# Strassen blocks of a float32 decoder trunk: three of the seven block products go through one PSUM bank, with the tokens' high and low parts in one 512-column matmul

## The chip, the cores and the metric

The kernel runs on one core of a Trainium2 chip. The metric is the device time of one execution in microseconds (us), the median over several runs; what is compared is the kernel before and the kernel with the change.

## What is computed

A causal decoder trunk with 512 tokens of width 1024, in float32. Four SwiGLU feed-forward stages stand around an attention and pooling mixer and an mLSTM mixer. The change touches the feed-forward stages alone, and in them the first two of the three matrix products:

```python
D_MODEL, SEQ = 1024, 512
D_FF = 256 * ((8 * D_MODEL // 3 + 255) // 256)     # 2816

def swiglu(x, w_gate, w_up, w_down):
    return (jax.nn.silu(x @ w_gate) * (x @ w_up)) @ w_down

x = x + FFN_RESIDUAL * swiglu(rms_norm(x, gain), w_gate, w_up, w_down)    # 4 times in the trunk
```

## The kernel before, in words

Features lie on the partitions and tokens along the free dimension. Every float32 operand is split into a high part and the rest (fp32r), and a product is the sum of three: high weight by high token, high weight by low token, low weight by high token. A plain product of a 128x1024 weight tile with 512 tokens is 8 x 3 matmuls of 512 columns.

D_FF is 22 tiles of 128 rows (`FT`). The first `PLAIN` of them in each stage (5, 4, 3, 3 in the four stages) are computed plainly. The other 17 + 18 + 19 + 19 = 73 go through `block(p)`: the pair (up tile p, gate tile p) is a 2 x 2 block matrix (up and gate by left and right half of the input features) and the tokens are cut into two halves of 256. Strassen's scheme in Winograd's form makes the four result quarters from seven products instead of eight, each of 4 feature tiles x 3 matmuls with 256 columns, 84 matmuls in all. The seven are called one, five, six, seven, three, and two plain ones for the right halves of up and gate. Sums of weights (`ASR`, split into `ASH` and `ASL`) are made ahead by an accumulating DMA that GpSimd issues (`add_pair`) and by VectorE (`sums_second`, `sums_third`, `sums_split`). Sums of tokens are in `BF` and `BFL`.

Between the products quarter results have to be added up. Before the change, ScalarE copies product one out of PSUM (`copy_one`), VectorE adds the others to it on the way to the small buffer MID (`mid_two`, `mid_five`, `mid_three`), and adds MID onto the up bank and the gate bank (`whole_up`, `whole_gate`). TensorE has the next product in other banks meanwhile.

Around a block stand these steps. ScalarE copies the high part of the next weights (`split`: HI<-RING, 1024 columns, then 512) and of the next sums (`sums_split`: ASH<-ASR, twice), and of a piece of the down weights (`early_split`: DHI<-DRAW). VectorE makes the low parts behind it (LO, ASL, DLO). When the block is done VectorE multiplies by the norm factor (`gate`), ScalarE applies Silu (`silu`), GpSimd multiplies again, VectorE multiplies by the up bank (`up`), ScalarE copies the high part (`h_high`: HH<-TMP), and GpSimd makes the low part. Behind most blocks TensorE runs `early(p)`: a part of the down product, 24 matmuls of 512 columns, or 18 with the first four pieces of stages two to four. It needs DHI and DLO of that block. The stages have 16 such pieces each. Block 15 of the third and fourth stage (`ALONE`) has none behind it, nor have the blocks 20 and 21 of stages two to four, nor block 21 of the first.

The order on each engine is written out by hand in the program, with semaphores between the engines. An engine carries out its own list in order, so an instruction that waits holds up all behind it.

## Time and profile before

| | |
|---|---|
| median of 3 runs | 1956.07 us (1955.17 to 1956.20) |
| span of the profiled execution | 1954.0 us |
| PE busy | 1948.1 us (100%), 11722 matmuls |
| VectorE (DVE) busy | 1397.9 us (72%) |
| ScalarE (ACT) busy | 851.6 us (44%) |
| GpSimd (POOL) busy | 527.3 us (27%) |
| granted TensorE clock | 1.000 |

The span reaches from the first to the last instruction of one profiled execution. The profile gives no other time for that execution, so the 2.1 us between the span and the median of the runs are what lies around it. A busy share is an average over all stages, and a matmul's recorded duration overlaps the next one's, so TensorE's pace is read from the starts of its matmuls.

### The profile page before, as it was taken

How to read it: one execution, taken by the hardware profiler on the slowest of the kernel's cores; microseconds unless marked ns; L12 is line 12 of the kernel's file. 1: busy time of each engine (PE TensorE's matmuls, PEld its weight loads, DVE VectorE, ACT ScalarE, POOL GpSimd, SP SyncE). 2: the span in 40 equal slices, each digit the busy share in tenths (PEclk: the TensorE clock that was granted, in tenths of full speed). 3: DMA queues.
4: the chain of work that ended last, by engine and by line, in shares of the span. 5: the costliest groups of instructions: out<-in, count | busy, mean ns of one | idle time of the engine just before them, and what ended most of it. 6: DMA issues, size and time to landing. Idle time of an engine off the chain costs nothing.

```text
span 1954.0 us, 28996 instructions
## 1 busy us (share of the span) xinstructions
PE 1948.1 (100%) x11722; PEld 1707.3 (87%) x11722; DVE 1397.9 (72%) x1882; ACT 851.6 (44%) x1230; POOL 527.3 (27%) x394
## 2 busy tenths in 40 slices
PE   9999999999999999999999999999999999999999
PEld 7999998877789999988999998877777888999997
DVE  7877776554588877768877776773458657877773
ACT  6443333535554344345433444442546345333431
POOL 1322222142223322223322322200015413322221
PEclk9999999999999999999999999999999999999999
DMA  6556663351346666545666653232200235666653
GB/s 211 155 164 171 173 168 95 119 181 55 88 126 176 174 172 167 147 129 145 178 166 172 181 151 114 97 96 88 76 1 1 87 116 160 177 173 168 178 141 107
DMA packets 112469, 265.92 MB, mean 136 GB/s; under 512 B 10321, under 2 KB 22865, under 8 KB 112337
## 3 DMA queue, kind: packets, MB, share of 16 engines
q1 hardware_dynamic: 92336, 225.72, 35.3%
q0 software_dynamic: 19856, 38.28, 12.5%
q8 instruction: 93, 1.52, 0.3%
q14 instruction: 40, 0.32, 0.0%
q10 hardware_dynamic: 144, 0.09, 0.0%
HBM read 259.32 MB, written 4.72 MB: 135 GB/s over the span
## 4 chain that ended last, share of the span: by engine, by line
PE 98%; DVE 1%; DMA 0%; issue 0%; ACT 0%; SPq 0%; POOL 0%; DVEq 0%
PE BANKS L656 12%; PE BANKS L658 12%; PE BANKS L657 12%; PE BANKS L579 11%; PE BANKS L580 11%; PE BANKS L581 11%; PE BANKS L709 6%; PE BANKS L710 6%; PE BANKS L711 6%; PE BANKS L1022 2%; PE BANKS L850 1%; PE BANKS L852 1%; PE BANKS L851 1%; PE BANKS L999 1%; PE BANKS L1005 1%; PE BANKS L813 1%
## 5 line engine op out<-in xcount | busy, mean ns | idle before, releaser
L656 PE MATMUL BANKS<-BF,ASH 128*128 128x256 f32 x876 | 248.0, 283 | 0.0
L658 PE MATMUL BANKS<-BF,ASL 128*128 128x256 f32 x876 | 247.9, 283 | 0.0
L657 PE MATMUL BANKS<-BFL,ASH 128*128 128x256 f32 x876 | 247.9, 283 | 0.0
L579 PE MATMUL BANKS<-XH,HI 128*128 128x512 f32 x624 | 245.7, 394 | 0.7 <-DVE XL L1593 0.3
L1657 DVE TENSOR_TENSOR LO<-RING,HI 128x1024 fp32r<-128x1024 f32 (+2 forms) x204 | 216.3, 1060 | 41.2 <-ACT HI L1160 39.9
L580 PE MATMUL BANKS<-XL,HI 128*128 128x512 f32 x624 | 243.2, 390 | 0.0
L581 PE MATMUL BANKS<-XH,LO 128*128 128x512 f32 x624 | 243.0, 389 | 0.0
L1173 ACT ACTIVATE TMP<-TMP 128x512 f32<-128x512 f32 x88 | 55.7, 633 | 406.4 <-DVE TMP L1686 406.4
L2262 POOL TENSOR_TENSOR TMP<-TMP,RSTD 128x512 f32<-128x512 f32 x88 | 132.0, 1499 | 365.3 <-ACT TMP L1173 365.3
L2254 POOL DMA_DIRECT2D ASR<-gu_dram x73 | 88.1, 1219 | 387.5 <-DMA ASR<-gu_dram 381.5
L709 PE MATMUL BANKS<-HH,DHI 128*128 128x512 f32 x488 | 190.7, 391 | 0.0
L710 PE MATMUL BANKS<-HL,DHI 128*128 128x512 f32 x488 | 190.6, 391 | 0.0
L1160 ACT ACTIVATE HI<-RING 128x1024 fp32r<-128x1024 f32 (+2 forms) x204 | 171.4, 876 | 42.3 <-DMA RING<-down_dram 21.4
L711 PE MATMUL BANKS<-HH,DLO 128*128 128x512 f32 x488 | 189.8, 389 | 0.0
L1676 DVE TENSOR_TENSOR ASL<-ASR,ASH 128x1024 fp32r<-128x1024 f32 x146 | 181.6, 1246 | 0.0
L2264 POOL TENSOR_TENSOR HL<-TMP,HH 128x512 fp32r<-128x512 f32 x88 | 139.0, 1580 | 146.6 <-ACT HH L1179 146.6
L1584 DVE TENSOR_TENSOR LO<-RING,HI 128x1024 fp32r<-128x1024 f32 x66 | 85.3, 1294 | 121.6 <-ACT HI L1102 121.5
L656 PEld LDWEIGHTS BANKS<-BF,ASH 128*128 128x128 f32 x876 | 168.2, 192 | 0.0
L657 PEld LDWEIGHTS BANKS<-BFL,ASH 128*128 128x128 f32 x876 | 168.2, 192 | 0.0
L658 PEld LDWEIGHTS BANKS<-BF,ASL 128*128 128x128 f32 x876 | 168.2, 192 | 0.0
L658 PE MATMUL BANKS<-XH,LO 128*128 128x256 f32 x584 | 165.3, 283 | 0.0
L657 PE MATMUL BANKS<-XL,HI 128*128 128x256 f32 x584 | 165.2, 283 | 0.0
(249 smaller groups left out, 4875.5 us busy)
## 6 DMA issues: line engine op xcount, KB each, us to landing
RING<-gu_dram SPq DMA_DIRECT2D x174, 512.0 KB, 3.9
ASR<-gu_dram SPq DMA_DIRECT2D x146, 256.0 KB, 2.9
ASR<-gu_dram POOLq DMA_DIRECT2D x73, 512.0 KB, 6.9
DRAW<-down_dram SPq DMA_DIRECT2D x40, 512.0 KB, 3.7
RING<-oin_dram SPq DMA_DIRECT2D x32, 512.0 KB, 3.5
RING<-down_dram SPq DMA_DIRECT2D x32, 384.0 KB, 3.2
DRAW<-down_dram SPq DMA_DIRECT2D x24, 384.0 KB, 3.7
RING<-ein_dram SPq DMA_DIRECT2D x16, 512.0 KB, 3.6
```

The costliest lines, as they stand in the source:

```text
L579: pe.matmul(PS[bank][:], HI[j][:, c], hi(k), start=(n == 0), stop=False)
L580: pe.matmul(PS[bank][:], HI[j][:, c], lo(k), start=False, stop=False)
L581: last = pe.matmul(PS[bank][:], LO[j][:, c], hi(k), start=False, stop=(n == len(order) - 1))
L656: pe.matmul(out, w_hi[:, c], x_hi(k), start=(k == 0), stop=False)
L657: pe.matmul(out, w_hi[:, c], x_lo(k), start=False, stop=False)
L658: last = pe.matmul(out, w_lo[:, c], x_hi(k), start=False, stop=(k == 3))
L709: pe.matmul(bank, DHI[:, col], HH[:, h % 8, :], start=(k == 0), stop=False)
L710: pe.matmul(bank, DHI[:, col], HL[:, h % 8, :], start=False, stop=False)
L711: last = pe.matmul(bank, DLO[:, col], HH[:, h % 8, :], start=False, stop=(h == tiles[-1]))
L1160: act.activation(HI[j][:, cols], RAW[j][:, cols], ACT.Copy).then_inc(hi_ready, 1)
L1657: dve.tensor_tensor(LO[j][:, cols], RAW[j][:, cols], HI[j][:, cols].bitcast(F32), ALU.subtract).then_inc(lo_ready, 1)
L1676: dve.tensor_tensor(ASL[:, p % 2, 2 * i:2 * i + 2, :], ASR[:, p % 2, 2 * i:2 * i + 2, :], ASH[:, p % 2, 2 * i:2 * i + 2, :].bitcast(F32), ...
```

## The change

Products one, six and seven now accumulate in one bank, `PS[4 + p % 2]`, without being cleared between. In them, high weight by high token and high weight by low token are one matmul of 512 columns instead of two of 256: its left half of the bank receives the high tokens' part, its right half the low tokens' part. For that, the high and low parts of the tokens lie in one tensor (`XHL`, and `BFHL` for the token sums). Low weight by high token stays a matmul of 256 columns into the left half. The other four products stay as they were. Product five goes into the right half of the up bank, and three and the right part of up are accumulated over it.

Since a bank runs on, its contents are taken between the products by ScalarE: both halves after one and after six (`copy_one`, `copy_six`, 512 columns each), five from the up bank to the gate bank (`copy_five`), and the right half after seven (`copy_seven`). TensorE waits for `one_copied` ahead of six, for `five_copied` ahead of the right part of up, and for `six_copied` ahead of seven. VectorE's three `mid_` additions go; `whole_up` is two additions of 512 columns, and `join_low` adds the two halves of the chained bank before `whole_gate`. The loads of the weight sums are issued after product seven instead of product five.

```diff
@@ TensorE @@
+                def chained(bank, w_hi, w_lo, tokens, fresh):
+                    parts = bank.rearrange("p (m t) -> p m t", m=2)
+                    for k in range(4):
+                        c = slice(k * P, k * P + P)
+                        both = tokens(k)
+                        pe.matmul(parts, w_hi[:, c], both, start=(fresh and k == 0), stop=False, skip_group_check=True)
+                        last = pe.matmul(parts[:, 0, :], w_lo[:, c], both[:, 0, :], start=False, stop=(k == 3),
+                                         skip_group_check=True)
+                    return last
...
-                    if g:
-                        pe.wait_ge(mid_made, 5 * g - 2)
-                    product(PS[5][:, low], HI[up][:, left], LO[up][:, left], plain(0, 0)).then_inc(one_done, 1)
+                    if g >= 2:
+                        pe.wait_ge(low_joined, g if p == PLAIN[f] else g - 1)
+                    chained(chain, HI[up][:, left], LO[up][:, left], plain(0, 0), True).then_inc(one_done, 1)
                     pe.wait_ge(sum_lo, 2 * g + 1)
-                    product(PS[4][:, low], *summed(p, 0), form(1)).then_inc(seven_done, 1)
-                    product(gate_bank[:, high], *summed(p, 1), form(0)).then_inc(five_done, 1)
+                    product(up_bank[:, high], *summed(p, 1), form(0), True, True).then_inc(five_done, 1)
                     pe.wait_ge(one_copied, g + 1)
                     pe.wait_ge(sum_lo, 2 * g + 2)
-                    product(PS[5][:, low], *summed(p, 2), form(2)).then_inc(six_done, 1)
-                    product(up_bank[:, low], HI[up][:, right], LO[up][:, right], plain(4, 0)).then_inc(unit_done, 1)
-                    product(up_bank[:, high], *summed(p, 3), plain(4, 1)).then_inc(three_done, 1)
-                    pe.wait_ge(mid_made, 5 * g + 2)
+                    chained(chain, *summed(p, 2), form(2), False).then_inc(six_done, 1)
+                    pe.wait_ge(five_copied, g + 1)
+                    product(up_bank[:, low], HI[up][:, right], LO[up][:, right], plain(4, 0),
+                            False, True).then_inc(unit_done, 1)
+                    pe.wait_ge(six_copied, g + 1)
+                    chained(chain, *summed(p, 0), form(1), False).then_inc(seven_done, 1)
+                    product(up_bank[:, high], *summed(p, 3), plain(4, 1), False, True).then_inc(three_done, 1)
@@ SyncE @@
-                        sp.wait_ge(five_done, block_count(f, n // 2 - 2) + 1)
+                        sp.wait_ge(seven_done, block_count(f, n // 2 - 2) + 1)
                         load_pair(f, n // 2)
@@ ScalarE @@
+                    act.activation(MIDS[:, :, 0, :], halves(PS[4 + p % 2]), ACT.Copy).then_inc(one_copied, 1)
+
+                def copy_five(p):
+                    up_bank, gate_bank = block_banks(p)
+                    act.wait_ge(five_done, block_count(f, p) + 1)
+                    act.activation(PS[gate_bank][:, TH_:T], PS[up_bank][:, TH_:T], ACT.Copy).then_inc(five_copied, 1)
+
+                def copy_six(p):
+                    act.wait_ge(six_done, block_count(f, p) + 1)
+                    act.activation(MIDS[:, :, 1, :], halves(PS[4 + p % 2]), ACT.Copy).then_inc(six_copied, 1)
+
+                def copy_seven(p):
+                    g = block_count(f, p)
+                    act.wait_ge(seven_done, g + 1)
+                    if g:
+                        act.wait_ge(low_joined, g)
+                    act.activation(MID[:, 4, :], PS[4 + p % 2][:, TH_:T], ACT.Copy).then_inc(seven_copied, 1)
...
                     copy_one(p)
                     if p == first:
                         h_high(p - 1)
+                        copy_five(p)
                         early_split(p)
                     elif not has_early(f, p - 1):
+                        copy_five(p)
                         h_high(p - 1)
                     if nxt:
                         split(2 * nxt, whole)
-                        split(2 * nxt + 1, right)
+                        if p > first and has_early(f, p - 1):
+                            copy_five(p)
+                            split(2 * nxt + 1, right)
+                            copy_six(p)
+                        else:
+                            copy_six(p)
+                            split(2 * nxt + 1, right)
                         sums_split(nxt, 0)
                         sums_split(nxt, 1)
...
+                    copy_seven(p)
                     if p == ALONE[f]:
                         early_split(p + 1)
                     elif has_early(f, p) and not leads(f, p):
@@ VectorE @@
+                    for part in range(2):
+                        if part:
+                            dve.wait_ge(up_added, 2 * g + 1)
+                        dve.tensor_tensor(bank, bank, MIDS[:, part, :, :], ALU.add).then_inc(up_added, 1)
+
+                def join_low(p):
+                    g = block_count(f, p)
+                    dve.wait_ge(seven_copied, g + 1)
+                    dve.tensor_tensor(MID[:, 5, :], PS[4 + p % 2][:, 0:TH_], MID[:, 4, :],
+                                      ALU.add).then_inc(low_joined, 1)
```

ScalarE's list between the end of one block and the next piece of down weights, in the repeating part of a stage. Here TMP<-TMP is `silu`, HH<-TMP is `h_high`, MID<-BANKS 128x256 is `copy_one`, HI<-RING are the next weights, ASH<-ASR the next sums and DHI<-DRAW is `early_split`. Before:

```order
L1173 ACTIVATE TMP<-TMP 128x512 [waits bank_free]
L1179 ACTIVATE HH<-TMP 128x512 [waits bank_free]
L1191 ACTIVATE MID<-BANKS 128x256 [waits mid_made,one_done]
L1160 ACTIVATE HI_56<-RING 128x1024 [waits weights_in2]
L1160 ACTIVATE HI_57<-RING 128x512 [waits weights_in3]
L1168 ACTIVATE ASH<-ASR 128x1024 [waits pair_sum1]
L1168 ACTIVATE ASH<-ASR 128x1024 [waits sum_made]
L1184 ACTIVATE DHI<-DRAW 128x1024 [waits early_in]
```

With the change (FORMS<-ASR is what was ASH<-ASR):

```order
L1191 ACTIVATE TMP<-TMP 128x512 [waits bank_free]
L1197 ACTIVATE HH<-TMP 128x512 [waits bank_free]
L1212 ACTIVATE MID<-BANKS 128x2x256 [waits up_added,one_done]
L1178 ACTIVATE HI_56<-RING 128x1024 [waits weights_in2]
L1217 ACTIVATE BANKS<-BANKS 128x256 [waits five_done]
L1178 ACTIVATE HI_57<-RING 128x512 [waits weights_in3]
L1221 ACTIVATE MID<-BANKS 128x2x256 [waits six_done]
L1186 ACTIVATE FORMS<-ASR 128x1024 [waits pair_sum1]
L1186 ACTIVATE FORMS<-ASR 128x1024 [waits sum_made]
L1228 ACTIVATE MID<-BANKS 128x256 [waits low_joined,seven_done]
L1202 ACTIVATE DHI<-DRAW 128x1024 [waits early_in]
```

Three copies out of a bank have come in, and the copy of the down weights (DHI) now stands behind the one that waits for product seven.

The first block of the first stage on ScalarE, with the change: `silu` of the last plain tile, then the block's copies.

```order
L1191 ACTIVATE TMP<-TMP 128x512 [waits bank_free]
L1212 ACTIVATE MID<-BANKS 128x2x256 [waits one_done]
L1197 ACTIVATE HH<-TMP 128x512 [waits bank_free]
L1217 ACTIVATE BANKS<-BANKS 128x256 [waits five_done]
L1202 ACTIVATE DHI<-DRAW 128x1024 [waits early_in]
L1178 ACTIVATE HI_54<-RING 128x1024 [waits weights_in0]
L1221 ACTIVATE MID<-BANKS 128x2x256 [waits six_done]
```

`copy_five` and `copy_six` stand behind `h_high` of the plain tile, and `copy_six` behind two more copies of 1024 columns; the first six of these rows but for `copy_five` stood in the same order before.

VectorE in the repeating part, before (DLO<-DRAW,DHI is the low part of the down weights, ASL<-ASR,ASH that of the sums, BANKS<-BANKS,MID first `whole_up`, then `whole_gate`, TMP<-BANKS,RSTD is `gate`):

```order
L1701 TENSOR_TENSOR MID<-BANKS,MID 128x256 [waits six_done,one_copied]
L1707 TENSOR_TENSOR MID<-BANKS,MID 128x256 [waits five_done,mid_made]
L1714 TENSOR_TENSOR MID<-BANKS,MID 128x256 [waits seven_done,mid_made]
L1737 TENSOR_TENSOR DLO<-DRAW,DHI 128x1024 [waits early_hi]
L1676 TENSOR_TENSOR ASL<-ASR,ASH 128x1024 [waits sum_hi]
L1724 TENSOR_TENSOR BANKS<-BANKS,MID 128x512 [waits three_done,mid_made]
L1731 TENSOR_TENSOR BANKS<-BANKS,MID 128x512 [waits unit_done,mid_made]
L1686 TENSOR_TENSOR TMP<-BANKS,RSTD 128x512 [waits mid_made]
```

With the change:

```order
L1776 TENSOR_TENSOR DLO<-DRAW,DHI 128x1024 [waits early_hi]
L1725 TENSOR_TENSOR FORMS<-ASR,FORMS 128x1024 [waits sum_hi]
L1763 TENSOR_TENSOR MID<-BANKS,MID 128x256 [waits seven_copied]
L1758 TENSOR_TENSOR BANKS<-BANKS,MID 128x512 [waits three_done,six_copied]
L1758 TENSOR_TENSOR BANKS<-BANKS,MID 128x512 [waits up_added]
L1770 TENSOR_TENSOR BANKS<-BANKS,MID 128x512 [waits unit_done,low_joined]
L1735 TENSOR_TENSOR TMP<-BANKS,RSTD 128x512 [waits gate_added]
```

The additions that led have gone; behind the low part of the sums there is one of 256 columns (`join_low`) and one more of 512.

## Rows read from the trace of the kernel before

**Rows 1.** The page, chain that ended last: shares by engine.
```profile
PE 98%; DVE 1%; DMA 0%; issue 0%; ACT 0%; SPq 0%; POOL 0%; DVEq 0%
```

**Rows 2.** Timeline of PE (start us, us, ...): a block, its early piece, the next block.
```profile
202.87 0.28 PE L656 MATMUL BANKS<-XH,HI 128*128 128x256 f32 x1
...
212.94 0.40 PE L709 MATMUL BANKS<-HH,DHI 128*128 128x512 f32 x1
...
218.41 0.28 PE L656 MATMUL BANKS<-XH,HI 128*128 128x256 f32 x1
```

**Rows 3.** Timeline of ACT in that block; idle time before it and its releaser in brackets.
```profile
204.50 0.38 ACT L1191 ACTIVATE MID<-BANKS 128x256 f32<-128x256 f32 x1 [1.73 <-PE BANKS L658]
204.78 1.57 ACT L1160 ACTIVATE HI<-RING 128x1024 fp32r<-128x1024 f32 x2
...
208.15 1.04 ACT L1184 ACTIVATE DHI<-DRAW 128x1024 fp32r<-128x1024 f32 x1
...
217.68 0.63 ACT L1179 ACTIVATE HH<-TMP 128x512 fp32r<-128x512 f32 x1 [2.37 <-DVE TMP L1695]
```

**Rows 4.** Timeline of DVE in the same block.
```profile
205.94 1.22 DVE L1657 TENSOR_TENSOR LO<-RING,HI 128x1024 fp32r<-128x1024 f32 x1 [0.20 <-ACT HI L1160]
...
209.69 0.41 DVE L1714 TENSOR_TENSOR MID<-BANKS,MID 128x256 f32<-128x256 f32 x1
210.02 1.22 DVE L1737 TENSOR_TENSOR DLO<-DRAW,DHI 128x1024 fp32r<-128x1024 f32 x1
211.16 1.22 DVE L1676 TENSOR_TENSOR ASL<-ASR,ASH 128x1024 fp32r<-128x1024 f32 x1
...
213.21 0.70 DVE L1731 TENSOR_TENSOR BANKS<-BANKS,MID 128x512 f32<-128x512 f32 x1 [0.23 <-PE BANKS L658]
213.95 0.69 DVE L1686 TENSOR_TENSOR TMP<-BANKS,RSTD 128x512 f32<-128x512 f32 x1
```

**Rows 5.** Groups of ACT by shape: count, busy us, mean ns, idle before.
```profile
L1184 ACT ACTIVATE DHI<-DRAW 128x768 fp32r<-128x768 f32 x12 | 10.0, 830 | 0.0
...
L1310 ACT ACTIVATE STG<-BANKS 128x512 f32<-128x512 f32 x8 | 4.8, 595 | 3.0 <-PE BANKS L646 3.0
```

**Rows 6.** Group of DVE by shape.
```profile
L1737 DVE TENSOR_TENSOR DLO<-DRAW,DHI 128x768 fp32r<-128x768 f32 x12 | 11.8, 987 | 0.0
```

**Rows 7.** Timeline of PE: first block of each stage, and block 15 of the third.
```profile
63.01 0.28 PE L656 MATMUL BANKS<-XH,HI 128*128 128x256 f32 x1
...
578.13 0.28 PE L656 MATMUL BANKS<-XH,HI 128*128 128x256 f32 x1
...
913.23 0.28 PE L656 MATMUL BANKS<-XH,HI 128*128 128x256 f32 x1
...
1094.27 0.28 PE L656 MATMUL BANKS<-XH,HI 128*128 128x256 f32 x1
...
1639.15 0.28 PE L656 MATMUL BANKS<-XH,HI 128*128 128x256 f32 x1
```

**Rows 8.** Timeline of ACT: `h_high` in the first block of each stage.
```profile
68.21 0.63 ACT L1179 ACTIVATE HH<-TMP 128x512 fp32r<-128x512 f32 x1 [1.86 <-DVE TMP L1695]
...
584.02 0.63 ACT L1179 ACTIVATE HH<-TMP 128x512 fp32r<-128x512 f32 x1 [1.85 <-DVE TMP L1695]
...
917.93 0.63 ACT L1179 ACTIVATE HH<-TMP 128x512 fp32r<-128x512 f32 x1 [1.86 <-DVE TMP L1695]
...
1641.94 0.63 ACT L1179 ACTIVATE HH<-TMP 128x512 fp32r<-128x512 f32 x1 [0.78 <-DVE TMP L1695]
```

**Rows 9.** Timeline of ACT behind block 15 of the third stage.
```profile
1106.36 0.63 ACT L1173 ACTIVATE TMP<-TMP 128x512 f32<-128x512 f32 x1 [5.77 <-DVE TMP L1686]
...
1109.13 0.63 ACT L1179 ACTIVATE HH<-TMP 128x512 fp32r<-128x512 f32 x1 [1.86 <-DVE TMP L1695]
```

**Rows 10.** The page, DMA issues of the weight sums: KB each, median us to landing.
```profile
ASR<-gu_dram SPq DMA_DIRECT2D x146, 256.0 KB, 2.9
ASR<-gu_dram POOLq DMA_DIRECT2D x73, 512.0 KB, 6.9
```

More of the change, by code:

```diff
@@ L650, in block_ffn, with product @@
                 base = 4 * q0
[L652 to L653 removed]
+                def product(out, w_hi, w_lo, tokens, fresh=True, shares=False):
                     for k in range(4):
                         c = slice(k * P, k * P + P)
[L656 to L658 removed]
+                        both = tokens(k)
+                        pe.matmul(out, w_hi[:, c], both[:, 0, :], start=(fresh and k == 0), stop=False,
+                                  skip_group_check=shares)
+                        pe.matmul(out, w_hi[:, c], both[:, 1, :], start=False, stop=False, skip_group_check=shares)
+                        last = pe.matmul(out, w_lo[:, c], both[:, 0, :], start=False, stop=(k == 3),
+                                         skip_group_check=shares)
+                    return last
[3 more added lines that the diff above has]
+                        c = slice(k * P, k * P + P)
+                        both = tokens(k)
+                        pe.matmul(parts, w_hi[:, c], both, start=(fresh and k == 0), stop=False, skip_group_check=True)
+                        last = pe.matmul(parts[:, 0, :], w_lo[:, c], both[:, 0, :], start=False, stop=(k == 3),
+                                         skip_group_check=True)
                     return last
@@ L1280, in block_ffn @@
                         split(NU, late)
+                        if has_early(f, p - 1):
+                            copy_five(p)
+                        copy_six(p)
                         split(NU + 1, late)
+                    copy_seven(p)
                     if p == ALONE[f]:
```

88 lines of the change are left out of this document (29 added, 59 removed).

## The prediction, made before the changed kernel had run

> **What bounds the kernel now.** I read first the shares of the chain that ended last: TensorE has 98% of it [rows 1]. So every microsecond that TensorE's stream loses or gains goes into the result, and other engines matter where TensorE would have to wait for them. Next the timeline of TensorE over one repeating block. The block's 84 matmuls of 256 columns take 212.94 - 202.87 = 10.07 us, 0.1199 each; the 24 matmuls of 512 columns of the early piece take 218.41 - 212.94 = 5.47 us, 0.2279 each [rows 2]. There is no gap, and the block comes round every 15.54 us. Last I read ScalarE and VectorE over the same block. Both have idle time, but it lies where they wait for TensorE or for the other [rows 3, 4]: what decides is at which moment of the block their work is due.
>
> I count time from a block's first matmul. For the lists of the engines I use distances between starts: an engine begins its next instruction about 0.09 to 0.10 before the recorded end of the one before (210.02 to 211.16 with 1.22 recorded [rows 4]; 204.50 to 204.78 with 0.38 [rows 3]). So 1024 columns hold VectorE for 1.14 and ScalarE for 0.95, 512 columns for 0.60 and 0.53, 256 for 0.33 and 0.28. ScalarE starts 0.31 after the start of the last matmul that it waits for: product one's last is 11 x 0.1199 = 1.32 behind 202.87, at 204.19, and the copy starts at 204.50 [rows 2, 3]. VectorE starts 0.11 after ScalarE's recorded end: 204.78 + 1.05 = 205.83, then 205.94 [rows 3, 4]. From ScalarE to TensorE no row shows a wait; I take 0.05, between 0 and that 0.11. TensorE's wait is due one matmul (0.12) ahead of the product, for the weight load.
>
> **What the matmuls give back.** In each of three products, four times two matmuls of 256 columns become one of 512: 2 x 0.1199 - 0.2279 = 0.012 each, 12 per block, 0.143 per block. The block becomes 60 x 0.1199 + 12 x 0.2279 = 9.93. Over 73 blocks: **-10.4 us**, and that is all there is to win, since the columns streamed stay the same. The Trainium skill (TensorE: Matmul & The Clock Gate, Back-to-back issue gap) gives an isolated warm matmul N/2.4 + 2.5 ns, so joining two would save 2.5 ns, 2.2 us over 876; the row's 12 ns is nearly five times that, and the row decides.
>
> In the new block product one ends at 1.39, five at 2.83, six at 4.22, right up at 5.66, seven at 7.05, three at 8.49, gate at 9.93.
>
> **The repeating block.** ScalarE's list now has `early_split` behind `copy_seven`, and VectorE's low part of it stands ahead of everything that finishes the block. Seven's last matmul starts at 6.93, so: `copy_seven` at 7.24, DHI at 7.52, its end at 8.56, DLO on VectorE at 8.67, low part of the sums 9.81, `join_low` 10.94, `whole_up` 11.27. Its second addition waits for the first, as `gate` does for `whole_gate` (0.74 [rows 4]): 12.01. Then `whole_gate` at 12.61. From `whole_gate` on nothing is changed: `h_high` followed 217.68 - 213.21 = 4.47 later [rows 3, 4], now at 17.08. Behind it ScalarE has `copy_one` of the next block: 17.61. A copy of 512 columns out of PSUM records 0.595 [rows 5]; with 0.05 the weights of product six may load at 18.26, and its first matmul starts at 18.38. That matmul stands 2.83 behind the block's start, so blocks can't follow closer than 15.55. TensorE's own work would be 9.93 + 5.47 = 15.40. **0.15 is lost in each**, all that the matmuls had given. (Before, `early_split` began at 5.28 [rows 2, 3], and product six had until 4.3.)
>
> This holds where DHI is made in the block before and has 1024 columns. Of 64 early pieces, 6 belong to blocks that have theirs made ahead (the first of each stage, and block 16 of stages three and four), 9 of the rest have 768 columns. 49 x 0.15 = **+7.3 us**.
>
> In those 9, DHI takes 0.21 less and DLO 0.23 less (0.830 against 1.04, 0.987 against 1.22) [rows 3 to 6], so the blocks can follow at 15.10. But the early piece has 18 matmuls there: 9.93 + 4.10 = 14.03. 9 x 1.07 = **+9.6 us**.
>
> **First blocks.** In a stage's first block `h_high` of the last plain tile, `copy_five`, `early_split` and the next weights stand ahead of `copy_six`. `h_high` starts at 5.20, 5.89, 4.70 and 2.79 in the four stages [rows 7, 8]; nothing ahead of it is changed. Then 0.53 + 0.28 + 0.95 + 0.95 + 0.595 + 0.05 = 3.36 in the first stage, and 0.21 less in the others (768 columns). Seven's weights are due at 5.54. The stalls are 3.0, 3.5, 2.3 and 0.4: **+9.2 us**. (They include those of six and of right up before them, which are smaller.)
>
> **Blocks without an early piece, followed by another block.** `silu` of block 15 starts 12.09 behind its start, and `h_high` 2.77 later [rows 7, 9]. Now three ends 0.14 earlier, and `whole_up` has 0.74 more: `silu` at 12.69. `copy_one` of the next block stands behind it: 13.22, done for TensorE at 13.87; due 9.93 + 2.71 = 12.64, 1.23 late. Then `h_high` at 15.46, next weights 15.99, `copy_six` 16.94, done 17.59; due 9.93 + 5.54 + 1.23 = 16.70, 0.89 late. 2.12 for block 15 in two stages; for block 20 in three stages 0.1 less (896 columns of weights). **+10.3 us.** The first stage has none: its block 20 has an early piece.
>
> **What I cost at nothing.** VectorE's total per block hardly changes (two of 0.33 out, one of 0.60 in). `copy_five` and `copy_six` in the repeating block: h_high starts 17.08 - 15.55 = 1.53 into the block, and with 0.53 + 0.50 + 0.95 of work `copy_five` runs at 3.51, `copy_six` at 4.45 when six is done. They are done 0.2 and 0.5 ahead of TensorE. If weights landed late by more, each microsecond would count.
>
> **Sum.** -10.4 + 7.3 + 9.6 + 9.2 + 10.3 = +26.0 on a span of 1954.0, so 1980.0; with the 2.1 around it, 1982.
>
> **Rivals.**
> 1. *The waits are covered, and only the matmuls count.* It needs TensorE to find the copies done although `h_high` stands ahead of them. For it speaks that ScalarE is busy 44% and that no product waits now. Against it, the dates above are starts of the trace and lists in order. 1956.1 - 10.4 = 1945.7. It decides if the chain from seven to `copy_one` is 0.15 shorter in 49 blocks and the 27 us of the other terms are mis-read too. 5%.
> 2. *The repeating blocks lose nothing and the first and last ones are half as bad*: -10.4 + 14 or so, about 1960 and down to no change. 7%, of which 4 within 0.2% and 1 faster.
> 3. *The weight sums come late.* Their loads are now issued behind seven, at 7.3 and 7.6 instead of 4.5, right ahead of 512 KB of other weights; GpSimd's accumulating DMA follows them and lands 6.9 after its issue [rows 10]. With 3.4 for the loads (2.9 and the issue) that is 18.0, or 2.4 into the next block. ScalarE needs them at 4.9, and VectorE must have made the next sum from them by 5.9, or `copy_seven` slips. The margin is about 2.4. If contention adds 3 us, the 58 blocks lose some 0.6 each and more in short ones: 1982 + 40 = 2020. The Trainium skill (DMA: Bandwidth & Descriptors, SWDGE vs HWDGE vs iDMA) says that the engines alternate between GpSimd's queue and SyncE's, which speaks for it, without a size. 10%.
> 4. The forecast: 78%.
>
> The errors of the forecast lie in the handovers: 0.05 in ScalarE to TensorE could be 0 to 0.11, over 58 repeating blocks -3 to +4; a copy of two halves of a bank may cost up to two of 256 columns (0.76 against 0.595), +0.17 x 58 = 10 more in the repeating blocks. ScalarE can't be shorter than one of 256 (0.38): -0.2 x 58 = -12. The likeliest one's own range is 1970 to 1994; with rivals 2 and 3 at the edges I take 1966 to 2000. Faster by over 0.2% (about what this kernel's runs can tell from no change): 6%; within: 4%; slower: 90%.
>
> **What the profile will show.** Right: about 10846 matmuls; the gap between the starts of blocks 15.5 in the repeating part with a short idle before product six (waiting for ScalarE's MID); 15.1 in place of 14.18 in the short ones; 2 to 3.5 us of idle in the first block of the first three stages ahead of seven; about 2 behind block 15 and 20. Wrong: blocks every 15.40 (then my chain is too long), or GpSimd's DMA as the releaser of ScalarE's sums with blocks over 16 (rival 3), or pairs of starts of chained matmuls that differ from 0.228 and 0.120 (then the strided token operand costs something, which no row shows; 0.01 on each of 876 would be 9 us).

## The result, and the profile after

| | before | changed |
|---|---|---|
| median of the runs made together | 1955.62 us (4 runs) | 1980.47 us (4 runs) |
| range | 1954.97 to 1956.20 | 1979.87 to 1981.72 |
| span of the profiled execution | 1954.0 us | 1980.0 us |

The changed kernel takes 1.0129 times as long, with a 95% interval of 1.0115 to 1.0144: slower by 1.3%, or 24.9 us between the medians. The span grew by 26.0 us, but the profiled execution is the longest of the four of the changed kernel (1981.72). In each of these four the time lies 1.7 to 1.8 us above the span of the same execution.

The page of the changed kernel, busy time and chain that ended last. They answer to [rows 1]:

```profile
PE 1953.6 (99%) x10846; PEld 1666.1 (84%) x10846; DVE 1381.5 (70%) x1809; ACT 951.9 (48%) x1449; POOL 525.4 (27%) x394
...
PE 82%; DVE 6%; ACT 3%; DMA 3%; issue 2%; POOL 2%; SPq 0%; DVEq 0%; ACTq 0%
```

There are 876 matmuls fewer, and still TensorE is the engine in which the time lies. But its share of the chain fell from 98 to 82%: it now waits. Which waits, says the view of TensorE's waits (us in total, times, longest):

```profile
PE BANKS L671 <- ACT MID L1212: 12.0, 16, 1.1
PE BANKS L671 <- ACT MID L1221: 4.7, 9, 0.7
PE BANKS L831 <- DVE SQB L1942: 2.0, 1, 2.0
PE BANKS L659 <- ACT BANKS L1217: 1.9, 3, 0.9
```

L671 is the joined matmul. In 16 cases product six waits for `copy_one` (L1212), in 9 product seven for `copy_six` (L1221), in 3 right up for `copy_five` (L1217), the copy out of the up bank. All three are copies that TensorE has to wait for since the change. L831 is a matmul of the attention mixer, which the change doesn't touch.

The timeline of TensorE in the block that answers to [rows 2], with its early piece and the next block:

```profile
205.36 0.39 PE L671 MATMUL BANKS<-XHL,HI 128*128 128x512 f32 x1
...
215.34 0.47 PE L727 MATMUL BANKS<-HH,DHI 128*128 128x512 f32 x1
215.65 0.39 PE L728 MATMUL BANKS<-HL,DHI 128*128 128x512 f32 x1
...
220.89 0.39 PE L671 MATMUL BANKS<-XHL,HI 128*128 128x512 f32 x1
...
222.29 0.28 PE L659 MATMUL BANKS<-FORMS 128*128 128x256 f32 x1
```

The block's matmuls take 215.34 - 205.36 = 9.98 us instead of 10.07; product one, with its joined matmuls, takes 222.29 - 220.89 = 1.40 (1.43 before). The early piece takes 5.55 instead of 5.47, because its second matmul starts 0.31 after the first and not 0.23. Together 15.53.

ScalarE and VectorE over the same block, against [rows 3, 4]:

```profile
206.90 0.63 ACT L1197 ACTIVATE HH<-TMP 128x512 fp32r<-128x512 f32 x1 [2.37 <-DVE TMP L1745]
207.44 0.58 ACT L1212 ACTIVATE MID<-BANKS 128x512 f32<-128x512 f32 x1
...
212.67 0.38 ACT L1228 ACTIVATE MID<-BANKS 128x256 f32<-128x256 f32 x1 [0.37 <-PE BANKS L672]
212.95 1.05 ACT L1202 ACTIVATE DHI<-DRAW 128x1024 fp32r<-128x1024 f32 x1
```

```profile
214.04 1.23 DVE L1776 TENSOR_TENSOR DLO<-DRAW,DHI 128x1024 fp32r<-128x1024 f32 x1 [2.29 <-ACT DHI L1202]
...
216.32 0.42 DVE L1763 TENSOR_TENSOR MID<-BANKS,MID 128x256 f32<-128x256 f32 x1
216.65 1.42 DVE L1758 TENSOR_TENSOR BANKS<-BANKS,MID 128x512 f32<-128x512 f32 x2
217.98 0.69 DVE L1770 TENSOR_TENSOR BANKS<-BANKS,MID 128x512 f32<-128x512 f32 x1
218.70 0.69 DVE L1735 TENSOR_TENSOR TMP<-BANKS,RSTD 128x512 f32<-128x512 f32 x1
```

The chain is there as forecast, from seven's copy at 7.31 into the block over DHI (7.59) and DLO (8.68) to `gate` (13.34). DLO's recorded end is 215.27, just ahead of the early piece that needs it, at 215.34. TensorE's second matmul there is 0.08 late. The view gives no wait at this place; that this is the mark of a late release is what runs 1 and 2 test (the last section has more of the mark).

The distances from block to block, in us, in place of [rows 7] (stage and block number):

| | before | changed |
|---|---|---|
| first blocks of stages 1 to 4 | 15.54, 14.26, 14.18, 14.18 | 18.18, 16.55, 15.27, 14.69 |
| stage 2, blocks 6, 7, 8 | 14.18, 14.18, 15.54 | 15.32, 14.99, 16.48 |
| repeating blocks | 15.54 | 15.53 to 15.55, two at 15.47, block 17 of stage 3 at 15.73 |
| block 16, stages 3 and 4 | 15.55, 15.55 | 17.48, 17.48 |
| block 21 to the next stage's, stages 2 and 3 | 81.43, 462.57 | 83.21, 464.34 |
| block 21 of stage 1 to the next stage's | 266.48 | 269.39 |

The last row holds the attention mixer: +2.9 us that nothing in the prediction names.

### The profile page after: what moved, and what is told of

The parts are those of the page before. It is cut to its first block, busy times and chain, and to the rows that moved or that the text cites. A ratio compares the mean times of both kernels' runs of the same rounds, so it can differ in the third digit from the quotient of the medians.

```text
span 1980.0 us, 27243 instructions
## 1 busy us (share of the span) xinstructions
PE 1953.6 (99%) x10846; PEld 1666.1 (84%) x10846; DVE 1381.5 (70%) x1809; ACT 951.9 (48%) x1449; POOL 525.4 (27%) x394
## 4 chain that ended last, share of the span: by engine, by line
PE 82%; DVE 6%; ACT 3%; DMA 3%; issue 2%; POOL 2%; SPq 0%; DVEq 0%; ACTq 0%
PE BANKS L582 9%; PE BANKS L671 9%; PE BANKS L583 9%; PE BANKS L584 9%; PE BANKS L661 6%; PE BANKS L662 6%; PE BANKS L659 6%; PE BANKS L727 5%; PE BANKS L729 5%; PE BANKS L728 5%; PE BANKS L672 4%; PE BANKS L1040 2%; POOL TMP L2288 2%; DMA RING<-gu_dram 2%; DMA ASR<-gu_dram 1%
## 5 line engine op out<-in xcount | busy, mean ns | idle before, releaser
L582 PE MATMUL BANKS<-XHL,HI 128*128 128x512 f32 x624 | 246.1, 394 | 0.8 <-DVE LO L2224 0.7
L583 PE MATMUL BANKS<-XHL,HI 128*128 128x512 f32 x624 | 243.7, 390 | 0.0
L584 PE MATMUL BANKS<-XHL,LO 128*128 128x512 f32 x624 | 243.3, 390 | 0.0
L671 PE MATMUL BANKS<-FORMS 128*128 128x512 f32 x584 | 215.4, 403 | 16.7 <-ACT MID L1212 12.0
L1725 DVE TENSOR_TENSOR FORMS<-ASR,FORMS 128x1024 fp32r<-128x1024 f32 x146 | 181.8, 1247 | 0.0
L1776 DVE TENSOR_TENSOR DLO<-DRAW,DHI 128x1024 fp32r<-128x1024 f32 (+1 forms) x64 | 75.7, 1182 | 130.8 <-ACT DHI L1202 130.8
L672 PE MATMUL BANKS<-FORMS 128*128 128x256 f32 x584 | 164.2, 281 | 0.0
L582 PEld LDWEIGHTS BANKS<-XHL,HI 128*128 128x128 f32 x624 | 117.4, 188 | 37.3 <-DVE LO L1633 6.0
L1186 ACT ACTIVATE FORMS<-ASR 128x1024 fp32r<-128x1024 f32 x146 | 146.7, 1051 | 3.1 <-DMA ASR<-gu_dram 1.7
L671 PEld LDWEIGHTS BANKS<-FORMS 128*128 128x128 f32 x584 | 110.0, 188 | 42.1 <-ACT MID L1212 15.3
L584 PEld LDWEIGHTS BANKS<-XHL,LO 128*128 128x128 f32 x624 | 117.4, 188 | 24.8
```

The source lines that it names most:

```text
L582: pe.matmul(PS[bank][:], HI[j][:, c], hi(k), start=(n == 0), stop=False)
L583: pe.matmul(PS[bank][:], HI[j][:, c], lo(k), start=False, stop=False)
L584: last = pe.matmul(PS[bank][:], LO[j][:, c], hi(k), start=False, stop=(n == len(order) - 1))
L671: pe.matmul(parts, w_hi[:, c], both, start=(fresh and k == 0), stop=False, skip_group_check=True)
L672: last = pe.matmul(parts[:, 0, :], w_lo[:, c], both[:, 0, :], start=False, stop=(k == 3), skip_group_check=True)
L1725: dve.tensor_tensor(ASL[:, p % 2, 2 * i:2 * i + 2, :], ASR[:, p % 2, 2 * i:2 * i + 2, :], ASH[:, p % 2, 2 * i:2 * i + 2, :].bitcast(F32), ...
```

## The experiments

All are variants of the changed kernel but the eighth. Every median stands beside runs of the kernel before made in the same session (medians 1954.78 to 1955.45); ratios are to those.

**1. DHI ahead of the copy of seven.** ScalarE's only change, in blocks whose early piece is their own:

```diff
+                    if has_early(f, p) and not leads(f, p):
+                        early_split(p)
                     copy_seven(p)
-                    elif has_early(f, p) and not leads(f, p):
-                        early_split(p)
```

> One move on ScalarE, in the repeating blocks alone: the high part of the down weights (DHI) is copied ahead of copy_seven instead of behind it. Theory of the chain (product seven, copy_seven, DHI, DLO, the rest of the block): DHI starts at about 6.8 instead of 7.6 into the block, DLO and all behind it 0.8 earlier; repeating blocks 15.40 apart instead of 15.53 (49 of them, -6.4 us) and the nine short ones at about 14.1 to 14.2 instead of 15.0 (-8); in all about -14, near 1966 us, first blocks and blocks without an early piece unchanged. Rival, the 512-column matmul with its two-part token operand costs the missing 0.13 us of each block itself: repeating blocks stay at 15.53, no more than -8 us, from the short ones.

Measured: 1972.31 us, ratio 1.0092 (1.0075 to 1.0108); span 1969.2.

The timelines of TensorE and ScalarE in its block, and TensorE's start of the next:

```profile
188.72 0.39 PE L671 MATMUL BANKS<-XHL,HI 128*128 128x512 f32 x1
...
195.56 1.04 ACT L1202 ACTIVATE DHI<-DRAW 128x1024 fp32r<-128x1024 f32 x1
...
204.17 0.39 PE L671 MATMUL BANKS<-XHL,HI 128*128 128x512 f32 x1
```

DHI starts 6.84 into the block instead of 7.59 (195.56 - 188.72), `gate` 12.59 instead of 13.34, and the repeating blocks come every 15.45 instead of 15.53. 15.45 is then their own pace, since no wait is left in them. The gain is smaller than expected because that pace is not 15.40, and because the short blocks (14.27, 14.65, 15.63 in stage two) kept some of their stalls.

**2. The next block's `copy_one` ahead of `h_high`.** `copy_one(p + 1)` is issued before `h_high(p)` and left out at the next block's head.

> One move on ScalarE: copy_one of the next block stands ahead of h_high of this one where the block has an early piece. Two chains leave product seven: one ends at product six of the next block (through h_high and copy_one), the other at the block's own early piece (through DHI and DLO). If, as the trace with the change shows, the early piece's wait for DLO is what costs 0.13 us in a repeating block, they stay at 15.53 apart; the nine short ones, whose idle time lies ahead of six, fall from 15.0 to 14.0 (-9 us), near 1971. Rival, the prediction's wording, by which the wait ahead of six sets both kinds: repeating blocks fall to 15.40 too, -15 us, near 1965.

Measured: 1975.03 us, ratio 1.0103 (1.0086 to 1.0120); span 1973.8. The repeating blocks stayed at 15.53, with the same 0.08 at the early piece's second matmul (0.31 behind the first, below); the short ones fell to 14.34, 14.35, 15.77, where 14.09, 14.09 and 15.45 would be without a stall. So the repeating blocks are held by DHI and DLO at their own early piece. `copy_one` behind `h_high`, which the prediction names as the place, holds the short ones only.

```profile
214.39 0.47 PE L727 MATMUL BANKS<-HH,DHI 128*128 128x512 f32 x1
214.70 0.39 PE L728 MATMUL BANKS<-HL,DHI 128*128 128x512 f32 x1
```

**3. First blocks.** `copy_one`, `copy_five` and `copy_six` go ahead of `silu` and `h_high` of the plain tile:

```diff
+                if f < 3:
+                    copy_one(first)
                 silu(first - 1, 1.0)
...
-                        h_high(p - 1)
                         copy_five(p)
+                        copy_six(p)
+                        h_high(p - 1)
                         early_split(p)
```

> ScalarE's order in the first block of each stage alone: copy_one ahead of silu of the last plain tile (not in the fourth stage), and copy_five and copy_six ahead of h_high, the down weights and the next weights (in the fourth stage h_high stays ahead of copy_six). Theory: the idle time of 2.8, 2.5, 1.2 and 0.7 us in these blocks goes, about -7 us, near 1973. Rival, given back: it only hid later waits, blocks behind the first get longer, less than -4 us.

Measured: 1979.07 us, ratio 1.0121 (1.0104 to 1.0138); span 1981.1. The first blocks ran at 15.45, 14.82, 14.09 and 14.09, and the blocks behind them at 16.55, 18.29, 15.94 and 14.96: given back. VectorE's list of the first block (DLO, two sums, two low parts, `join_low`) starts later behind the later DHI, so `gate`, `silu` and `h_high` are late, and `copy_one` of the next block stands behind them. The 18.29 has a second part, which the windows show (columns: stretch, busy us of PE, PEld, DVE, ACT and POOL with counts, granted clock, DMA share, GB/s):

```profile
601.00:603.00 2.00, 0.04 (x1) 0.00 (x0) 1.41 (x3) 0.69 (x2) 0.55 (x1) 1.00 0.15 46
603.00:604.00 1.00, 0.52 (x3) 0.48 (x4) 1.00 (x3) 1.00 (x2) 0.98 (x1) 1.00 0.02 6
604.00:605.00 1.00, 1.00 (x8) 0.86 (x8) 1.00 (x2) 1.00 (x3) 0.62 (x1) 1.00 0.00 0
605.00:606.00 1.00, 1.00 (x7) 1.00 (x6) 0.93 (x3) 1.00 (x3) 0.00 (x0) 0.52 0.00 0
606.00:607.00 1.00, 1.00 (x7) 1.00 (x6) 1.00 (x1) 1.00 (x2) 0.00 (x0) 0.50 0.02 8
```

TensorE waited 2.4 us for `copy_one`, and 1.5 us after it had restarted the granted clock fell to 0.50 (1.2 GHz, the lower of its two levels) for over 3 us; 256 columns then take 0.21 instead of 0.12. That costs 1.5 us on top of the wait. The clock also fell near the start of this profile, at 7.7, behind a wait of 1.9 us for a low part of weights.

**4. Blocks behind block 15 and 20.** There `copy_one` goes ahead of `silu`, and `copy_six` ahead of `h_high` and the weights.

> ScalarE's order around the blocks without an early piece (15 and 20) alone: copy_one of the following block ahead of silu, and its copy_five and copy_six ahead of h_high. Theory: the idle time of 1.9 to 2.1 us in blocks 16 and 21 goes, five times, about -9.5 us, near 1971. Rival: silu and h_high come later instead and the last product of the stage waits for them, less than -5 us.

Measured: 1974.62 us, ratio 1.0099 (1.0082 to 1.0116); span 1974.0. That is 5.9 us less than the changed kernel, where 9.5 were expected. Block 16 fell to 15.46 and 15.45, and the term of block 21 is gone (81.27, 462.68). But in stage three block 17 took 19.27 (and in stage four 15.95). VectorE's timeline in stage three, at the end of block 16:

```profile
1128.06 0.69 DVE L1718 TENSOR_TENSOR ASR<-ASR,RING 128x512 f32<-128x512 f32 x1 [2.82 <-DMA ASR<-gu_dram]
```

The sums of weights, whose loads are issued only after product seven, came late, everything behind them in VectorE's order too, and TensorE waited 2.0 us until 1139.08, followed by over three microseconds at a granted clock of 0.50. This is rival 3 of the prediction. Some 24 repeating blocks of this profile ran at 15.47 and not 15.53, with their wait still there (their early piece's second matmul is 0.06 late); that is 1.5 us of the gain which the moved copies do not explain.

**5. All four moves.**

> The four moves on ScalarE together (DHI ahead of copy_seven, copy_one ahead of h_high, the first blocks' order, the order around blocks 15 and 20). Alone they measured, against the changed kernel's 1980: -7.7, -5, -1 and -5.4. Theory: TensorE's waits for ScalarE's copies nearly vanish, but the weight sums that now are loaded after product seven arrive late in short blocks and in the blocks behind first blocks and behind block 15, as two of the four runs showed; about 1960 to 1965. Rival, the waits for ScalarE were all there was: 1980.5 minus the idle times, 1948 to 1950.

Measured: 1956.64 us (10 runs, 1953.80 to 1961.84), ratio 1.0010 (1.0000 to 1.0019); span 1954.2. Repeating blocks 15.45, short ones mostly 14.09. That is neither of the two values expected (1960 to 1965, and 1948 to 1950). What TensorE still waits for beside the mixer:

```profile
PE BANKS L659 <- ACT BANKS L1217: 2.8, 4, 1.2
```

These are four blocks, behind a first one, a short one or block 16 (15.54, 15.25, 16.11, 15.97), where `copy_five` is late behind `h_high` and the weights. The mixer lost 3.1 us.

**6. and 7. The matmuls split again**, in the changed kernel (6) and with all four moves (7), nothing else altered:

```diff
-                        pe.matmul(parts, w_hi[:, c], both, start=(fresh and k == 0), stop=False, skip_group_check=True)
+                        pe.matmul(parts[:, 0, :], w_hi[:, c], both[:, 0, :], start=(fresh and k == 0), ...)
+                        pe.matmul(parts[:, 1, :], w_hi[:, c], both[:, 1, :], start=False, ...)
```

> The changed kernel with each 512-column matmul of a chained product split again into two of 256 columns into the same two halves of the bank; all waits, copies and orders stay. It prices the matmuls alone. A product of the chain then takes 12 x 0.12 = 1.44 us; the traces show 1.41 for the joined one, where the prediction had 1.39. In the repeating blocks the chain from seven contains six's and seven's products of the next block, so they grow by about 0.06 to 0.1, to 15.6. In all +4 to +8 us, 1985 to 1988. Rival, by the prediction's 0.012 per matmul and a bound wholly on TensorE: +10 us.

> The kernel with the four moves, with the joined matmuls split again. There TensorE is the bound in nearly all blocks, so the difference to the kernel with the four moves is the price of the matmuls: 73 x 0.09 = 6.5 us if a joined product takes 1.41, 73 x 0.143 = 10.4 us if it took the 1.39 of the prediction.

Measured: 1983.41 us, ratio 1.0142 (1.0125 to 1.0159), span 1982.7, and 1960.67 us, ratio 1.0029 (1.0017 to 1.0041), span 1958.1. In run 7 undelayed blocks take 15.54 and 10.07 where run 5 has 15.45 and 9.99: joining is worth 0.085 to 0.09 per block, not 0.143. Over 73 blocks that is 6.2 to 6.5 us. The difference of the kernels is smaller (3 and 4 us, under the 4 to 8 expected of run 6 and the 6.5 of run 7), since in the two with split matmuls the mixer lost nothing (266.55 and 266.48).

**8. The kernel before, with the loads of the weight sums issued later**, after the right part of up instead of product five (two products, 2.9 us).

> The kernel before with one part of the change alone: the loads of the weight sums are issued when the right part of up is done (7.2 us into a block) instead of after product five (4.5), about where the change puts them (7.1); nothing else differs. Theory: in the repeating blocks of 15.54 us GpSimd's accumulating DMA has landed in time and nothing moves; in the short ones VectorE waits for it but TensorE hardly does; 0 to +5 us, from block 17 of stages three and four and the blocks behind the first ones. Rival (the late sums carry much of the 25 us that the change lost): +10 us or more.

Measured: 1957.05 us, ratio 1.0010 (1.0000 to 1.0020). The repeating blocks stayed at 15.54; a first block lost 0.8 and five short ones 0.1 to 0.5 each; the span is 1.3 us longer.

**9. The mixer.** In the changed kernel the matmul at L831 waits because the last weights of the mixer landed late. The DMA view of that load, 428.0 to 433.2 us (busy tenths of the DMA engines, then the queues):

```profile
DMA  0000009993249948967651001000000000000000
...
q1 hardware_dynamic: 144, 0.52, 33.3%
q8 instruction: 1, 0.02, 1.3%
...
RING<-ein_dram SPq DMA_DIRECT2D x1, 512.0 KB, 5.1
```

One load of instructions is in it, and it lands after 5.1 us. In the profiles of the kernel before and of runs 6 to 8 no load of instructions is within 4 us of that one, and ScalarE waits 4.3 to 4.5 us for these weights. In runs 1 to 5, as in the changed kernel, one starts between 425 and 430, and ScalarE waits 6.2 to 6.5. So I moved it: the kernel of run 5, with product one of stage one split again, 68 matmuls more ahead of the mixer.

> The kernel with all four moves, but in stage one alone product one splits its joined matmul in two again (68 matmuls more). In the profiles of the changed kernel and of every variant that lost 3 us in the attention mixer, one load of instructions (a queue of the kind instruction, 16 KB) starts between 425 and 430 us, while the last weights of the mixer are being loaded, and that load ends with packets trickling in one by one; where the mixer lost nothing the load of instructions lies at least 6 us away from it. Theory code: TensorE's instructions are fetched in pieces, and 136 instructions more (68 matmuls, 68 weight loads) ahead of the mixer make the piece start some 15 us earlier, at about 410; the mixer weights then land 1.5 to 2 us sooner, the distance from block 21 of stage one to the next stage falls from 269.56 to 266.5, and the time is that of the kernel with four moves less 3 and plus 0.5 for the split matmuls: about 1954 us. Rival chance: the late landing has another reason (the phase of the memory, joined matmuls as such), and the distance stays at 269.5, the time at 1957.

Measured: 1955.22 us (11 runs), ratio 1.0001 (0.9992 to 1.0010); span 1952.9. The load of instructions starts at 413.0, the weights land as before the change:

```profile
RING<-ein_dram SPq DMA_DIRECT2D x1, 512.0 KB, 3.5
```

ScalarE waits 4.9 us and the mixer takes 266.42. The median fell by 1.4 and not by 2.6; other blocks lost in this profile (stage four: 14.59, 15.73 and 15.99). The intervals of runs 5 and 9 overlap, so that the mixer got its time back is read from the distance, and not from the medians.

**10. One of the two loads of a pair earlier**, after product five, the other after seven as before; otherwise run 9.

> The kernel of the run before, and of the two loads of a pair of weight sums the one whose place product five reads is issued as soon as five is done, the other as before after seven. Theory loads late: what still holds the blocks behind a first or a short one (1.4, 1.1, 2.0 and 0.5 us over their own pace) is that the sums' chain starts only after product seven; the second load of 256 KB alone should land some 0.5 us sooner than the two together (3.1 us in the median), so these four blocks lose about 0.5 us less each: 1 to 2 us less than the run before, about 1952.5. Rival queue: the early load takes its place in front of nothing and the late one still takes 3 us, since landing time is fixed cost rather than bytes: the time stays within 0.3 us of the run before.

Measured: 1953.92 us (11 runs), ratio 0.9992 (0.9983 to 1.0001); span 1952.9. In its profile the blocks that run 9 loses in stages three and four are on pace again, apart from 15.25, 14.27 and 15.53. One block of stage two got worse, 17.61: TensorE waited 1.8 us for `copy_five`, and the clock was granted at 0.50 from 598.5 on. It has the lowest median of all variants, 1.3 us under run 9's as expected, but the intervals of the two overlap, and its own still includes the time before.

**11. and 12. The same load of instructions moved towards the weights**: run 7 with product one joined in 13 blocks of stage one (11), or in all 17 (12).

> The kernel with all four moves and every matmul split (no loss in the mixer: 266.48), but product one of the first 13 blocks of stage one uses the joined matmul (52 matmuls fewer). Theory code: 104 instructions fewer move the piece of code that was fetched at 413.9 to about 425 or 426, into the load of the last mixer weights, and the mixer loses some 3 us although the kernel has hardly a joined matmul: distance 269 to 269.6, time about 1963 (1960.7 less 0.4, plus 3). Rival: lateness comes with the joined matmuls as such or by chance of the phase; the distance stays 266.5 and the time 1960.3.

> In the run before, the piece of code was fetched at 423.1 us, in the gap between two loads of mixer weights, and the mixer lost nothing (distance 266.5): it missed the window of the last load, from 424.6 to about 428. Here product one uses the joined matmul in all 17 blocks of stage one (16 matmuls fewer than before, some 32 instructions), everything else is split as before. Theory code: the fetch moves by 3 to 4 us to 426 or 427, the last weights land late, the distance becomes 269 to 269.6 and the time 1962.5 to 1963.5. Rival (the joined matmuls that the late runs had in common, or the phase of something else): distance 266.5, time 1960.2.

Measured: 1960.35 us, ratio 1.0026 (1.0016 to 1.0035), and 1960.86, ratio 1.0027 (1.0016 to 1.0039). The load of instructions came at 423.0 and 423.6, in both cases before the last weights' load was issued (424.3 and 423.8). It moved by 0.6 us between them instead of 3 to 4, so it doesn't follow the count of matmuls simply. The mixer lost nothing (266.52, 266.44). Neither run put it to the test.

## Why the prediction was right, and where its terms were not

The forecast of 1982.0 met 1980.47, and its +26.0 on the span met +26.0. The median rose by 24.9: the prediction put 2.1 us around the span where every execution for which both are on record has 1.7 to 1.8, and the profiled execution is the longest of its four. Term by term, in us (stalls measured as distance less the undelayed pace of 15.45, 14.09 or 9.98):

| term | predicted | measured |
|---|---|---|
| matmuls joined | -10.4 | -6.4 |
| repeating blocks | +7.3 | +3.8 |
| short blocks | +9.6 | +9.5 |
| first blocks | +9.2 | +7.0 |
| behind block 15 and 20 | +10.3 | +10.1 |
| attention mixer | 0 | +2.9 |

The rest is -0.9, of which 0.3 is a wait of the kernel before that went away behind the first block of stage two. The exact sum is partly luck. The matmuls gave 4.0 less than forecast, and the repeating blocks lost 3.5 less, which is mostly the same error seen twice; but the first blocks (2.2 less) and the mixer (2.9 more) have nothing to do with each other, and they cancel.

**Matmuls: mis-sized.** The prediction took 0.2279 for the joined matmul, the pace where the tokens are one contiguous row [rows 2]. Product one takes 1.40, so a joined matmul 1.40 / 4 - 0.1199 = 0.230; with split matmuls it takes 1.43 (run 7, and the kernel before), so 0.008 is saved by each. By the blocks of runs 5 and 7 the saving is 0.0875 / 12 = 0.007 each instead of 0.012. The prediction had named this among its signs of being wrong, pairs of starts that differ from 0.228 and 0.120 because of the tokens in two pieces; it came true, at 0.005 a matmul or 4 us. The rule of the Trainium skill (TensorE: Matmul & The Clock Gate, Back-to-back issue gap) for an isolated warm matmul, a fixed 2.5 ns each, would make it 2.2 us in all, an estimate: the runs lie between it and the row.

**Repeating blocks: the chain right, the place wrong.** Every date of the chain was met within 0.07 (copy of seven 7.24 and 7.31, DLO 8.67 and 8.68, `gate` 13.35 and 13.34, `copy_one` 17.61 and 17.61), and the blocks come at 15.53 where 15.55 was forecast. But the wait stands at the early piece, for DLO, and not ahead of product six. DLO ends 9.91 into the block and the early piece needs it at 9.98: a second deadline on the same chain, which the prediction didn't read. Run 1 takes DHI forward and the loss is gone; run 2 takes `copy_one` forward and it stays. The term is 3.8 and not 7.3 mostly since the undelayed pace is 15.45 and not 15.40, which is the error of the matmuls again (0.05 of the 0.07 a block); the rest is 15.53 in place of 15.55.

**The handover from ScalarE to TensorE: right.** No row had shown it when the prediction took 0.05. In the changed kernel TensorE's matmul starts 0.05 to 0.06 behind the recorded end of the copy that it waited for (589.34 behind 588.92 + 0.37). The 0.12 for the weight load isn't seen ahead of that matmul; the next one is 0.10 late instead, so the sum of the two was nearly right.

**Short blocks and blocks behind 15 and 20: right,** in place and size. Run 2 takes most of the first away (0.25 to 0.3 of about 0.9 a block is left), run 4 all of the second, but for what the late sums then cost in block 17.

**First blocks: mis-sized in stages two and three** (2.5 and 1.2 where 3.5 and 2.3 were forecast). The prediction took the starts of `h_high` from the trace before (5.20, 5.89, 4.70), since "nothing ahead of it is changed". That was true of the lists and not of the times. The timeline of ScalarE in stage two's first block of the changed kernel, which began at 583.48:

```profile
588.39 0.63 ACT L1197 ACTIVATE HH<-TMP 128x512 fp32r<-128x512 f32 x1 [1.64 <-DVE TMP L1745]
588.92 0.37 ACT L1217 ACTIVATE BANKS<-BANKS 128x256 f32<-128x256 f32 x1
589.22 0.82 ACT L1202 ACTIVATE DHI<-DRAW 128x768 fp32r<-128x768 f32 x1
589.95 1.04 ACT L1178 ACTIVATE HI<-RING 128x1024 fp32r<-128x1024 f32 x1
590.90 0.57 ACT L1221 ACTIVATE MID<-BANKS 128x512 f32<-128x512 f32 x1
```

`h_high` is at 4.91 and not 5.89. The elementwise engines come into this block 4.37 us later than before the change (588.39 - 584.02 [rows 8]), TensorE 5.35 (583.48 - 578.13 [rows 7]), so they have 0.98 in hand. In the plain tiles ahead they don't run on TensorE's beat: the `h_high` ahead of this one is later by the same amount (580.53 against 576.17). From `h_high` on the steps were as forecast.

But this date is not a fixed one. In runs 2, 4 and 6, whose order in this block is the same, `h_high` starts at 6.32, 6.36 and 6.43, TensorE waits earlier in the block, and the block takes 17.95, 18.01 and 18.09 instead of 16.55. From block 21 of stage one to block 5 of stage two it is 287.40 us in run 2 and 285.94 in the changed kernel. So the term of stage two lies between 2.4 (run 1) and 3.9 from profile to profile, with the forecast's 3.5 inside; the prediction took it as one number, and what sets the date is open.

**The mixer: missed.** The wait of 2.0 us at L831, which ended at 436.86, is followed by a fall of the clock, in the windows of the changed kernel:

```profile
435.00:436.00 1.00, 0.00 (x0) 0.00 (x0) 1.00 (x1) 0.31 (x1) 0.92 (x2) 1.00 0.73 102
436.00:437.00 1.00, 0.14 (x2) 0.17 (x3) 1.00 (x3) 0.00 (x0) 1.00 (x1) 0.82 0.93 332
437.00:438.00 1.00, 1.00 (x5) 0.78 (x6) 0.59 (x4) 0.00 (x0) 0.92 (x2) 0.50 0.24 90
438.00:439.00 1.00, 1.00 (x3) 0.74 (x3) 1.00 (x6) 0.88 (x4) 0.92 (x2) 0.50 0.00 0
439.00:440.00 1.00, 1.00 (x4) 0.78 (x3) 1.00 (x2) 0.00 (x0) 0.92 (x2) 0.50 0.00 0
```

The kernel before waits 0.2 us at this place. So some 1.8 of the 2.9 us are wait, and the other 1.1 go with the slower clock. Run 1 has the two apart: nearly the same wait (1.8), the clock at 1.00 throughout, and the mixer 1.5 longer than before (268.00). That the late weights come from the load of instructions is supported by 14 profiles (late in the six where it starts between 425 and 430, inside the load of the last weights; on time in the other eight) and by run 9, which changed nothing but stage one's matmuls and removed both. Runs 11 and 12 were to bring the loss about and didn't reach the place, so the opposite direction stays open. One more sign of it is in the profiles: in the kernel before and in run 8 the load of instructions starts 1.1 to 1.2 us into an earlier 512 KB load of the mixer's weights (408.3 and 407.1, 407.2 and 406.1), which then lands after 4.3 us; in run 6, without it, the same load takes 3.4.

**The rivals.** Rival 1 (only the matmuls count) is out: the waits are in the view. Rival 2 had no loss in the repeating blocks and the other terms half as large (+14); the repeating blocks lost 3.8 and the others 26.6. Rival 3 (late weight sums) has a small part in the changed kernel's time. VectorE waits 25.2 us in all for them, in 26 cases (4.7 in 5 before the change), mostly inside time that it had to spare. But in block 5 of stage two and block 4 of stage three the sums hold up the copy of seven, as the prediction had described for this rival:

```profile
945.79 0.69 DVE L1713 TENSOR_TENSOR ASR<-ASR,RING 128x512 f32<-128x512 f32 x1 [2.87 <-DMA ASR<-gu_dram]
...
947.25 1.06 ACT L1186 ACTIVATE FORMS<-ASR 128x1024 fp32r<-128x1024 f32 x1 [0.46 <-DVE ASR L1719]
948.21 0.36 ACT L1228 ACTIVATE MID<-BANKS 128x256 f32<-128x256 f32 x1
```

The block began at 940.25, so `copy_seven` is at 7.96 instead of 7.31. Blocks 4 and 5 of stage three take 14.32 and 15.42, where 14.09 and 15.01 would do, and block 6 of stage two takes 15.32 instead of 14.99: about 1 us in all, a tenth of what the table counts for the short blocks. Run 4 shows it larger, when the spare time is used up. Run 8 prices the later loads in the kernel before, which has no `copy_seven` behind them: 1.3 us on the span.

**Where the expected gain went.** The joined matmuls are worth 6.4 us at most. The order of the copies on ScalarE took 30 us away (3.8 + 9.5 + 7.0 + 10.1); putting a few of them elsewhere gave 24 back (run 5 against the changed kernel). What is left is at the level of the kernel before: 1.0010, and 1.0001 and 0.9992 with runs 9 and 10. No version is shown to beat it.

## What to carry to other kernels

When a bank runs on across products, each copy out of it becomes a deadline of TensorE on an in-order engine. Write down for every such copy what stands ahead of it in that engine's list, and date it in the repeating part, the first block and the last; the repeating part lost 4 us here, the edges 27. Take every consumer of a delayed chain into the account, not only the last one: here the early piece's need of DLO came due before product six. And count on a wait of some 2 us on TensorE to cost up to nearly twice its length, for the slower clock that may follow it.

## What the runs showed of the hardware

- TensorE waits 13 times for 1.6 to 2.4 us in the profiles of the changed kernel and its variants. At nine of them the granted clock fell from 1.00 to 0.50 (1.2 GHz) for over 3 us, from 0.2 us before to 1.6 us after the engine started again: in the changed kernel at 437, in runs 2 to 5 at the same place of the mixer, in run 3 also at 7.7 and 605, in run 4 at 1139, in run 10 at 598.5. That cost 1.1 to 1.7 us on top of the wait. Behind the other four (run 1, 1.8 us; run 3, 1.6; runs 11 and 12, 1.7) it stayed at 1.00, and so it did behind the waits of up to 1.1 us in the feed-forward stages of the changed kernel.
- The ten executions of run 5 lie 8 us apart where those of the kernel before lie 2 apart, and their mean granted clock goes with the time: 1.000 in the three of 1953.80 to 1955.23 us, 0.999 in four of 1955.97 to 1957.34, 0.998 in three of 1957.68 to 1961.84. One fall as above is 0.001 of the span. It isn't the only cause of spread: in run 7 the clock is 1.000 in all seven, and they lie 4 us apart.
- The first matmul after a wait starts on time, and the next about 0.1 us late, over and above its length (0.10 or 0.11 at each wait of 587, 589 and 591 us in the changed kernel).
- A joined matmul with tokens in two pieces takes 0.230 us in product one and 0.233 over the whole block, where one with 512 contiguous columns takes 0.228 and two of 256 take 0.240. In some stretches (blocks 8 and 9 of stage four of the changed kernel, most of stage one in run 4) the block's matmuls take 9.95 and not 9.98 us in the same order; why is open.
- A load of instructions (16 KB) that fell into a load of 512 KB of weights went with a landing time of 5.1 us instead of 3.5.
- A copy of both halves of a bank (512 columns) takes ScalarE 0.57 to 0.60, as a plain one does [rows 5].
